# One row of the samples' cached attention beside each of the prompt's heads, rotary columns projected twice, and the convolution state stored whole

## What is computed

```
q = (rms_norm(c_q) @ w_uq).reshape(b, s, 8, 64 + 32)      # 8 heads: 64 plain columns, 32 rotary ones
q_nope, q_pe = q[..., :64], rope(q[..., 64:], pos)
k_pe = rope(k_pe, pos); ckv = rms_norm(c_kv)              # 256 latent columns, one rotary key of 32
q_abs = einsum('bshn,chn->bshc', q_nope, w_uk)
# prompt: 4 blocks of 128 queries; block i attends causally to keys of blocks 0..i
# samples: the keys are 16 cached pages of 128 tokens, found through page_table, then the 4 new tokens
sc = (q_abs @ kc.T + q_pe @ kp.T) * 96 ** -0.5
p = softmax(where(kpos <= qpos, sc, NEG)); o_lat = p @ kc
o = einsum('bshc,chv->bshv', o_lat, w_uv)
mixer = concatenate([conv_out, o]) @ w_out
# rope(x): [x1*cos - x2*sin, x2*cos + x1*sin], x1 and x2 the two halves of the 32 columns
# also returned: the last two columns of the convolution's input of each sample (conv_sample)
```

## Time and profile before

| | us |
|---|---|
| median of three runs | 2348.23 (2346.67 to 2349.3) |
| the profiled execution, its own time | 2344.28 |
| its span, first to last instruction | 2342.6 |
| TensorE busy | 2204.5 |
| VectorE busy | 1029.6 |
| ScalarE busy | 699.7 |
| GpSimd busy | 279.7 |

### The profile page before, as it was taken

How to read it: one execution, slowest core, us unless ns; L and a number is a source line. 1 busy time by engine, 2 the same in 40 slices (tenths; PEclk the granted TensorE clock), 3 DMA queues, 4 the chain that set the end, 5 groups by cost and what they waited for, 6 DMA issues and landing times.

```text
span 2342.6 us, 41476 instructions
## 1 busy us (share of the span) xinstructions
PE 2204.5 (94%) x16722; PEld 2079.0 (89%) x16722; DVE 1029.6 (44%) x1279; ACT 699.7 (30%) x897; POOL 279.7 (12%) x289
## 2 busy tenths in 40 slices
PE   7999999998999999999999999998864599999997
PEld 7999999995999999999999999996520289999997
DVE  5442445466544334464433446665510054433443
ACT  5431222234254222234412222222510025522221
POOL 1001002100410000030000013030025240000002
PEclk9999999997999999999999999999975689999999
DMA  3244222220232222322222223233177322232221
GB/s 123 90 100 122 90 90 90 99 94 1 67 108 93 91 77 90 101 68 92 89 91 81 90 96 94 87 62 92 47 208 215 92 91 90 81 99 81 90 96 68
DMA packets 69014, 217.80 MB, mean 93 GB/s; under 512 B 10733, under 2 KB 23213, under 8 KB 68848
## 3 DMA queue, kind: packets, MB, share of 16 engines
q1 hardware_dynamic: 59440, 191.91, 25.3%
q0 software_dynamic: 9488, 24.71, 4.2%
HBM read 211.88 MB, written 5.71 MB: 93 GB/s over the span
## 4 chain that ended last, share of the span: by engine, by line
PE 86%; DVE 4%; DMA 3%; issue 3%; ACT 2%; SPq 2%; POOLq 1%; POOL 0%; DVEq 0%; ACTq 0%
PE ps L546 80%; DMA raw<-down 1%; SPq L444 1%; DVE rinv L1241 1%; PE ps L844 1%; DMA raw<-w_uq 1%; DVE w_lo L1231 1%; SPq L426 1%; PE ps L782 1%; POOLq L426 1%; DMA keys<-pool_kt 1%; ACT prob L1062 1%; ACT p_mla L1159 0%; PE ps L634 0%; PE ps L795 0%
## 5 line engine op out<-in xcount | busy, mean ns | idle before, releaser
L546 PE MATMUL ps<-hx_hi,w_hi 128*128 128x272 f32 x3376 | 702.7, 289 | 15.4 <-DVE hx_lo L1252 13.0
L546 PE MATMUL ps<-hx_hi,w_lo 128*128 128x272 f32 x3376 | 699.6, 289 | 0.0
L546 PE MATMUL ps<-hx_lo,w_hi 128*128 128x272 f32 x3376 | 696.9, 288 | 0.0
L995 ACT ACTIVATE w_hi<-raw 128x1024 fp32r<-128x1024 f32 (+2 forms) x299 | 334.7, 1119 | 1204.8 <-PE ps L546 1171.7
L546 PEld LDWEIGHTS ps<-hx_hi,w_hi 128*128 128x128 f32 x3376 | 531.8, 188 | 19.4 <-issue 14.4
L546 PEld LDWEIGHTS ps<-hx_lo,w_hi 128*128 128x128 f32 x3376 | 531.5, 189 | 0.0
L546 PEld LDWEIGHTS ps<-hx_hi,w_lo 128*128 128x128 f32 x3376 | 527.9, 189 | 0.0
L1231 DVE TENSOR_TENSOR w_lo<-raw,w_hi 128x1024 fp32r<-128x1024 f32 (+2 forms) x299 | 420.7, 1407 | 126.0 <-ACT w_hi L995 125.8
L546 PE MATMUL ps<-hid_hi,w_hi 128*128 128x272 f32 x1408 | 292.2, 289 | 4.1 <-DVE w_lo L1231 4.1
L546 PE MATMUL ps<-hid_lo,w_hi 128*128 128x272 f32 x1408 | 291.9, 288 | 0.0
L546 PE MATMUL ps<-hid_hi,w_lo 128*128 128x272 f32 x1408 | 291.5, 288 | 0.0
(11 more groups left out here) (277 smaller groups left out, 1619.7 us busy)
## 6 DMA issues: line engine op xcount, KB each, us to landing
raw<-gu SPq DMA_DIRECT2D x176, 512.0 KB, 3.2
raw<-down SPq DMA_DIRECT2D x64, 704.0 KB, 4.0
keys<-pool_kt SPq DMA_DIRECT2D x128, 144.0 KB, 3.7
vals<-pool_v POOLq DMA_DIRECT2D x128, 128.0 KB, 3.3
raw<-odd_in SPq DMA_DIRECT2D x21, 512.0 KB, 3.2
raw<-even_in SPq DMA_DIRECT2D x14, 512.0 KB, 3.2
raw<-even_out SPq DMA_DIRECT2D x8, 512.0 KB, 3.2
raw<-odd_out SPq DMA_DIRECT2D x8, 512.0 KB, 3.2
```

What stands on the lines that cost most here:

```text
L546: last = pe.matmul(acc[slot][0:m, a, 0:TH], w, r[:, t, a * TH:(a + 1) * TH], start=(begin and t == tiles[0] and one == 0), stop=(end and t ...
L995: act.activation(w_hi[slot][:, 0:cols], raw[slot][:, 0:cols], ACT.Copy).then_inc(w_hi_done, 1)
```

## The change

- **Order.** `attend()` replaces the loop over heads and `sample()`. In step h TensorE does the transposes of head h, the scores of head h+1, the transposes of row h-1, the scores of row h, the values of head h and the values of row h-1. Rows 0 to 3 belong to the first four samples, rows 4 to 7 to the others.
- **Running softmax.** Each row has its own maximum against the one so far (`row_maximum`), its exponentials, and its product is added to an accumulator that is scaled first (`row_add`). The new tokens start the accumulator, before the first head.
- **PSUM.** The prompt's scores are packed into three banks, the transposes of a head share one bank (three rounds, each waiting for ScalarE's copy of the one before), a row has banks 5 (scores), 6 (transposes) and 7 (values).
- **Slots.** 6 for keys, 8 for values. Value slots 4 to 7 lie over heads 0 to 3 of the prompt's queries and keys and are loaded as each of these is scored.
- **Rotary columns.** `w_uq` panels are 128 wide: a head's 96 columns, and its 32 rotary columns once more with the halves swapped. VectorE multiplies both by cosines and sines that carry the norm, and adds. `rotate` and `perm` are gone.
- **State.** All six columns of each sample are stored in one run per partition, and the caller takes the last four of them apart. The state comes in as one load and four small VectorE copies.
- **Output panels.** The first two also do the prompt's half of the attention tiles early (`out_begin`), so the late part is one half of the columns.

```diff
-K_SLOTS = 8
-V_SLOTS = 9
+ALL_ROWS = GROUPS * ROWS
+K_SLOTS = 6
+V_SLOTS = 8
+HEAD_SLOTS = 4
...
-            if u == 6:
-                eng.wait_ge(w_lo_done, ODD_OUT + 2)
-            if u == 7:
-                eng.wait_ge(mla_scored, BLOCKS * HEADS)
             if u >= K_SLOTS:
                 before = u - K_SLOTS
-                eng.wait_ge(scored[before % GB], before // (ROWS * GB) * (ROWS + 1) + before // GB % ROWS + 1)
+                eng.wait_ge(scored[before % GB], scored_after(before // GB))
...
-            if u == 2:
+            if u == 3:
+                eng.wait_ge(kf_ready, HEADS // 2)
+            if 4 <= u < 4 + HEAD_SLOTS:
                 eng.wait_ge(qa_done, 1)
-                eng.wait_ge(mla_scored, BLOCKS * HEADS)
+                eng.wait_ge(mla_scored, BLOCKS * (u - 3))
...
+            def attend():
+
+                for h in range(HEADS):
+                    mla_turn(h, 0)
+                    if h + 1 < HEADS:
+                        mla_score(h + 1, 0, 1)
+                    mla_turn(h, 1)
+                    if h + 1 < HEADS:
+                        mla_score(h + 1, 1)
+                    mla_turn(h, 2)
+                    if h:
+                        turn_row(h - 1)
+                    score_row(h)
+                    mla_values(h)
+                    if h:
+                        value_row(h - 1)
+                    if h == ROWS + 1:
+                        turn_latents(0)
+                turn_row(ALL_ROWS - 1)
+                out_begin(0)
+                value_row(ALL_ROWS - 1)
+                out_begin(1)
+                turn_latents(1)
...
                 for h in range(HEADS):
                     n = ODD_UQ + h
+                    if h == 0:
+                        link(dve.tensor_tensor(sin[QK:P, :], sin[QK:P, :], gate[QK:P, :], ALU.mult))
+                        link(dve.tensor_tensor(gate[NOPE:QK, :], gate[NOPE:QK, :], cos[NOPE:QK, :], ALU.mult))
...
                     dve.wait_ge(panel_done, n + 1)
-                    dve.tensor_tensor(halves(qf[0:QK, h, :]), acc_of(n % 2, QK), halves(gate[0:QK, :]), ALU.mult).then_inc(acc_read, 1)
+                    dve.tensor_tensor(halves(qf[0:QK, h, :]), acc_of(n % 2, QK), halves(gate[0:QK, :]), ALU.mult)
+                    dve.tensor_tensor(halves(silu[NOPE:QK, :]), ps[QK:P, 2 * (n % 2):2 * (n % 2) + 2, 0:TH], halves(sin[QK:P, :]), ALU.mult)\
+                       .then_inc(acc_read, 1)
                     split_next(n)
...
+            def row_add(r):
+
+                g, c = r // ROWS, r % ROWS + 1
+                o, l, al = o_acc[g][:], s_l[:, g:g + 1], s_al[:, g, c:c + 1]
+                for b in range(GB):
+                    dve.wait_ge(valued[b], valued_after(r))
+                dve.wait_ge(s_added, r + 1)
+                dve.scalar_tensor_tensor(out=l, in0=l, scalar=al, in1=s_sum[:, g, c:c + 1], op0=ALU.mult, op1=ALU.add)
+                dve.scalar_tensor_tensor(out=o, in0=o, scalar=al, in1=ps[:, 7, 0:KV_LORA], op0=ALU.mult, op1=ALU.add).then_inc(s_added, 1)
...
-            pool.dma_start(d["o_convs"], conv_zs[:, :, :, DS:DS + 2]).then_inc(stored_conv, 16)
+            pool.dma_start(d["o_convs"], conv_zs[:]).then_inc(stored_conv, 16)
```

More of the change, by code:

```diff
@@ L532, in _, with panel @@
         def _(pe):
-            def panel(n, slot, rhs_hi, rhs_lo, tiles, wait_input=None, m=P, begin=True, end=True):
+            def panel(n, slot, rhs_hi, rhs_lo, tiles, wait_input=None, m=P, begin=True, end=True, token_halves=(0, 1), stop=None):
                 if begin:
@@ L544, in panel @@
                     for w, r, one in ((hi, rhs_hi, 0), (hi, rhs_lo, 1), (lo, rhs_hi, 2)):
-                        for a in range(2):
+                        for a in token_halves:
                             last = pe.matmul(acc[slot][0:m, a, 0:TH], w, r[:, t, a * TH:(a + 1) * TH],
-                                             start=(begin and t == tiles[0] and one == 0), stop=(end and t == tiles[-1] and one == 2))
+                                             start=(begin and t == tiles[0] and one == 0),
+                                             stop=((end if stop is None else stop) and t == tiles[-1] and one == 2))
                 if end:
@@ L745, in even @@
                 mixer_out(EVEN_OUT, SGU_TILES, SWA_TILES, EVEN_PIECES)
-            def rotate(src, h):
-                for a in range(2):
-                    last = pe.matmul(ps[NOPE:QK, 6 + a, 0:TH], perm[NOPE:QK, :], src[NOPE:QK, a * TH:(a + 1) * TH],
-                                     start=True, stop=True)
-                last.then_inc(rotated, 1)
             def nope_keys(p):
@@ new lines, in turn_new_probs, with new_values @@
+            def turn_new_probs():
+                pe.wait_ge(new_exp, GROUPS)
+                for g in range(GROUPS):
+                    last = pe.transpose(ps[0:NS, 5, g * P:(g + 1) * P], p_n[:, g, :], ident[:])
+                last.then_inc(new_turned, 1)
+            def new_values():
+                pe.wait_ge(new_copied, 2)
+                for g in range(GROUPS):
+                    for b in range(GB):
+                        q = NS * b
+                        pe.matmul(ps[q:q + NS, 5, g * KV_LORA:(g + 1) * KV_LORA], p_st2[:, g, q:q + NS], ckv_new[:], start=True, stop=True)                          .then_inc(valued[b], 1)
@@ L889, in page_values, with value_row @@
+            def value_row(r):
+                pe.wait_ge(s_copied, r + 1)
+                pe.wait_ge(s_added, r + 1)
+                for k in range(4):
+                    u = 4 * r + k
                     pe.wait_ge(vals_landed[u % V_SLOTS], 64 * (u // V_SLOTS + 1))
                     for b in range(GB):
-                        r = NS * b
-                        pe.matmul(ps[r:r + NS, 7, 0:KV_LORA], p_st[:, p, r:r + NS], vals[u % V_SLOTS][:, b, :], start=(p == 0), stop=False)\
-                          .then_inc(valued[b], 1)
@@ L894, in page_values @@
[L894 to L897 removed]
+                        q = NS * b
+                        pe.matmul(ps[q:q + NS, 7, 0:KV_LORA], p_st[:, k, q:q + NS], vals[u % V_SLOTS][:, b, :],
+                                  start=(k == 0), stop=(k == 3)).then_inc(valued[b], 1)
             def turn_latents(g):
@@ L1874, in layout @@
     k0 = 3 * c_w + Q_LORA + KV_LORA
-    order = np.concatenate(tiles + [np.arange(3 * c_w, k0)] + [np.arange(k0, k0 + ROPE)] * 4)
+    turned = np.r_[ROPE // 2:ROPE, 0:ROPE // 2]
+    order = np.concatenate(tiles + [np.arange(3 * c_w, k0)] + [np.arange(k0, k0 + ROPE)] * 3 + [k0 + turned])
     a["odd_in"] = panels(w[:, order])
     a["odd_out"] = panels(i["odd_w_out"][0])
-    a["w_uq"] = panels(i["mla_w_uq"][0], QK)
+    heads = [np.r_[h * QK:(h + 1) * QK, h * QK + NOPE + turned] for h in range(HEADS)]
+    a["w_uq"] = panels(i["mla_w_uq"][0][:, np.concatenate(heads)])
     a["q_gain"], a["kv_gain"] = features(i["mla_q_norm"][0]), features(i["mla_kv_norm"][0])
```

411 lines of the change are left out of this document (200 added, 211 removed).

## The result

The changed kernel takes **2239.2 us** (median of 4 runs, 2238.01 to 2240.74), a ratio of **0.9534 [0.952, 0.9548]** to the kernel before: 109 us less. The profiled execution took 2240.28 us with a span of 2238.6 us. The forecast was 2251 (2228 to 2278), faster with 0.97.

A forecast was written before the change was run, and what follows sets the result against it. Two neighbouring stages with opposite limits, heads leaving DMA idle and cached attention paced by loads. Profiled 2344.28 less 97.6 (panel 2 earlier) plus 0.7 gives 2247.4; the median's 3.9 more makes 2251, range 2228 to 2278.

The forecast's parts named there:

- A, the panels: w_uq panels: 17.3 us removed, key projections at 1603.9, loads from 1609.4; 8 us back if the load stays late.
- B, the first head: Between first scores and first head: samples' own keys and values add 5.1 us; first head at 1644, 13 earlier.
- C, the steps: Merged heads and rows: loads 16.5 us a step, TensorE 12 and waiting about 4; values end at 1779.4.
- the formula: GpSimd's value queue from row 2: end at 1681.6 + 23p, p the pitch per unit, taken as 4.25: 1779.4.
- The other sign: Profile after, merged steps: DMA above 240 GB/s from 1660 to 1775.
- D, the tail: From last values to panel 2: 15.5 us against 14.3 before; panel 2 at 1794.9, 97.6 less.
- E, the rest: Four linked copies at the odd layer's start cost +0.7 us; state load, running maxima and adds hidden.
- Loads at their floor: Rival in the merged steps: p = 3.79 and full clock in the tail (12.5), giving 2238; chance 0.13.
- TensorE paces: Rival in the merged steps: clock falls in load waits and stays down, 17.7 us a step, about 2272; chance 0.20.
- Blocked issue: Rival in GpSimd's value issue: each transfer waits 0.47 us for VectorE, p = 5.7, giving 2285; chance 0.06.
- The w_uq load late: Rival at the w_uq panels: the load stays late though the store is contiguous, giving 2259; chance 0.05.
- slower: Rival in the merged steps: a row's loads begin only after the row before, 41 us a step, 2410; chance 0.02.

The follow-up runs named there:

- the relieved one: Changed kernel, page numbers of two units read at once on SyncE and GpSimd, ScalarE issuing the fourth batch's value page from row 2: 2233.11 us, ratio 0.9516.
- half reads: Changed kernel with two page-number reads per unit of four transfers, in keys and values: 2235.68 us; with half the value bytes too: 2226.39 us.
- the pair: Changed kernel with both half the page-number reads and half the bytes of every value transfer: 2226.39 us, ratio 0.9487.

## Why the prediction was right

**What bounded it.** Two neighbouring stages with opposite limits, one made of both: 91 us are left when the store and the projection are taken out, and the windows show where (50.6 + 177 us became 128.3). How much of the 91 is the new tail or the running softmax was not separated.

**A, the panels.** Key projections at 1604.95 (forecast 1603.9), first scores 1613.12 (1612.6), first page load 1610.74 (1609.4); w_uq loads at 2.9 us. One wait of 0.42 us stands in the panels, at VectorE's split behind its reciprocal of 3.56; the forecast had 0.3. The price put on a late load, 8 us, was too small in the changed kernel: it measured 13. The panels moved by 11 of it. In the kernel before, the same store cost 4.

**B, the first head.** 1641.13 against 1644: from the first scores to there took 28.0 us, not 31.4. It turned out to matter little: the first head started at 1642.10 in the second profile of the same kernel and at 1646.31 in the relieved one, which ended earlier than both. Loads were under way all along.

**C, the steps.** The starts of the heads are 8.5, 14.0, 15.7, 17.4, 17.4, 21.6 and 15.7 us apart, and 17.9 us lie between the last head's start and the last row's turn. The forecast had 16 to 18. From the second start on the mean is 17.1, of which the waits for keys are 2.5 and TensorE's own part 14.6, where the forecast had 4 and 12: it had the sum nearly right from two terms that were not. What it left out is the low clock right behind the waits. Four rows of TensorE's timeline, 18 products with keys each:

```profile
1656.71 2.76 PE L889 MATMUL ps<-keys,qa 96*32 96x512 f32 x18 [1.44 <-DMA keys<-pool_kt]
1670.72 4.46 PE L889 MATMUL ps<-keys,qa 96*32 96x512 f32 x18 [2.14 <-DMA keys<-pool_kt]
1705.54 4.46 PE L889 MATMUL ps<-keys,qa 96*32 96x512 f32 x18 [2.79 <-DMA keys<-pool_kt]
1724.25 5.33 PE L889 MATMUL ps<-keys,qa 96*32 96x512 f32 x18 [4.27 <-DMA keys<-pool_kt]
```

In six of the seven steps with such a wait these products take 4.14 to 5.33 us instead of 2.76. The step of 21.6 us holds the longest wait, 4.27, and the slowest work behind it.

GpSimd's queue: row 2's first unit at 1672.74 (1675.5), 4.08 a unit (4.25), the last values done at 1776.3 (1779.4), 3.1 us early. That time is in part luck. The start was 2.8 early and the 23 units 3.9 shorter, but the last values ended 7.4 behind the last issue where the formula had 3.8: pages landed in 4.8 and not 3.3, and TensorE came to them only behind the first half-panel. And in this profile TensorE waited for keys and never for values, so the formula follows a queue that was not the one waited for. It is not all luck: the last unit of values is issued at 1766.6 to 1768.8 whatever is done to keys, to bytes or to TensorE's work, and when keys came sooner the waits moved to values at the end. What the prediction had wrong is "loads pace" as one limit; bytes and issue stand at nearly one height, and neither alone decides.

**A ceiling of 270 GB/s.** The earlier trace rows gave 270 in 5 us; over 95 us the changed kernel had 261 and 267, the one with half reads 274, the relieved one 280. The ceiling was put at least 10 GB/s too low. The share of 1.00 at 261 GB/s and of 0.98 at 280 also says that a full share is not yet the highest rate. The other sign, over 240 GB/s from 1660 to 1775, was missed narrowly with 236.

**D, the tail.** 12.2 us against 15.5. The half-panel took 4.72 where 6.5 was put for a falling clock, and latents with output and lower half took 2.6 from 1781.04 to 1783.68 where 3.9 was summed. Together with C that is 104.0 for 97.6.

**E, the rest.** The four copies run for 0.81 us in all and stand in the chain: from the start of the layer's first small matmuls to its first panel are 8.17 us (1443.45 to 1451.62), 7.34 before (1443.74 to 1451.08), so they cost 0.83 where 0.7 was put. They lie ahead of panel 2, so the 104.0 holds them already. And the 3.9 added for the median over the profiled time didn't hold: the median after is 1.1 below the profiled run. From 2251.3 down to 2239.2 are 12.1: 3.8 of the stretch up to the last values (3.1, and the 0.7 for copies that its measured time includes), 3.3 of D and 5.0 of that offset. The offset is the difference of runs of one kernel, not of the change.

**The rivals.** *Loads at their floor* gave the closest time, 2238, for a reason that was not its own: p was 4.08, not 3.79, and only the tail's full clock came true. Its ground was misread, too: before did not keep 3.79 for twenty units; from 1754.35 to 1812.73 its 15 units took 3.89 in the mean. *TensorE paces*, with its 0.66 or 0.5 throughout, didn't occur: the clock fell in and behind single waits (0.50 from 1725 to 1730) but was 0.87 in the mean, and 1.1 us less of work in a step changed nothing. The Trainium skill (TensorE: Matmul & The Clock Gate, "HAM oscillation — how this bites in real kernels") describes a kernel in which each load wait sends the clock down; the trace agrees for six of the seven waits over 1 us, and the mean of 0.87 says that the clock came back between them. *Blocked issue* falls: most units took 3.79 us with VectorE busy for 36.75 of 95 us, and 3.37 with half reads beside 38.48. One unit did take 5.96, but the same unit took 5.87 in the kernel before (1859.19 to 1865.06), where VectorE did nothing from 1855 to 1866. For the same reason the 0.2 a unit that the prediction put on VectorE is not shown. The Trainium skill (SBUF — State Buffer, "SBUF: two separate sides") would have transfers wait for VectorE's two-port operations; GpSimd's issues show no such wait, and whether the landing time of 4.8 us holds one no run here separates. *The w_uq load late* and *slower* didn't occur.

## What to carry to other kernels

Two neighbouring stages, one waiting for transfers and one leaving them idle, can be worth more merged than repaired: some 91 us here, against 16 for two repairs. Once merged, take the limits away one at a time and then together; a zero for each one alone doesn't say that neither counts, it may say that both stand at one height, and only the pair shows the 12 us. A repair ahead of a stage that loads pace can be partly swallowed by it, so its price must be measured in the kernel that it is for (4 us in one, 13 in the other).

## What the hardware did that was not expected

- The pause in which GpSimd reads page numbers into registers does not follow their number: it is 1.20 us between units with two numbers, 1.66 with three (in the kernel where ScalarE issues the fourth page) and 1.50 with four. In the relieved kernel it is 2.66 for the eight of two units and 0.20 before the second, 2.86 in all, where two readings of four take 3.00: reading ahead for two units saves GpSimd little. Four rows of its timeline, the third behind a wait for a free slot:

```profile
1709.45 1.71 POOL L491 DMA_DIRECT2D vals<-pool_v  x3 [2.66 <-issue]
1711.36 1.71 POOL L491 DMA_DIRECT2D vals<-pool_v  x3 [0.20 <-issue]
1717.00 1.71 POOL L491 DMA_DIRECT2D vals<-pool_v  x3 [3.93 <-PE ps L928]
1718.91 1.70 POOL L491 DMA_DIRECT2D vals<-pool_v  x3 [0.20 <-issue]
```

- ScalarE issues one page transfer in 0.34 us of its queue and four, with a register read each, in 3.45 (4.54 the first time), where GpSimd takes 0.54 for one. Its pages took 6.6 us to land where GpSimd's took 5.0 in the same kernel; why was not tried.

```profile
1753.87 3.45 ACTq L491 DMA_DIRECT2D vals<-pool_v  x4
```

- Two profiles of the same kernel differ by 4.6 us in span (2238.6 and 2234.0) while their medians agree within 0.6: the third panel starts at 1788.53 in one and 1783.92 in the other. A difference of 2 to 5 us between two profiles is no evidence by itself.
